# Tanh for SiLU, three scores ahead, and work moved between blocks in a hybrid decoder layer

## The reference, cut to what matters

```
h = x*(1+sc1) + sh1                      # adaLN; sh, sc, gt from c @ w_ada + b_ada
qkv_a, z_a, b_a, a_a, q_b, k_b, v_b, f_b, g_a, g_b = split(h @ w_in)
qkv_a = silu(causal_conv4(qkv_a))        # branch A: gated delta net, 8 heads of 64
q_a, k_a = l2norm(q_a)/8, l2norm(k_a);  o_a = gdn(...);  o_a = rmsnorm(o_a)*silu(z_a)
o_b = softmax(q_b.k_b/8 + F_t - F_s) v_b # branch B: forgetting attention, causal
merged = sigmoid(g_a)*(o_a @ w_ba) + sigmoid(g_b)*(o_b @ w_bb)
x = layernorm(alpha*x + gt1*(merged @ w_out));  h2 = x*(1+sc2) + sh2
x = layernorm(alpha*x + gt2*moe(h2))     # 64 experts, top 8, and a shared one
```

## Time and profile before

| | us |
|---|---|
| median of three runs | 1819.17 |
| profiled execution | 1827.16 |
| its span, first to last instruction | 1825.4 |
| TensorE busy in the span | 1644.6 (90%) |
| VectorE, ScalarE, GpSimd busy | 668.7, 340.9, 323.0 |
| mean granted clock of TensorE | 0.945 of full speed |
| attention block, 163.9 to 340.3 | 176.4 |
| sample-attention block, 340.3 to 487.8 | 147.5 |
| norms block, 487.8 to 512.0 | 24.2 |
| delta-net block, 512.0 to 869.6 | 357.6 |
| gated-norm block, 869.6 to 887.7 | 18.1 |
| gating block, 887.7 to 958.3 | 70.6 |
| output block up to the expert loop, 958.3 to 1142.5 | 184.2 |
| expert loop and end, 1142.5 to 1825 | 682.5 |

### The profile page before, as it was taken

One profiled execution on the slowest core, in us unless ns is written; L12 is line 12 of the kernel. 1 busy time (PEld: TensorE's weight loads), 2 busy tenths in 40 slices (PEclk: granted clock), 3 DMA queues, 4 the chain that ended last, 5 costly groups with the idle time before them and its releaser, 6 DMA issues. The chain is left out here.

```text
span 1825.4 us, 19720 instructions
## 1 busy us (share of the span) xinstructions
PE 1644.6 (90%) x7369; PEld 952.1 (52%) x7369; DVE 668.7 (37%) x1267; ACT 340.9 (19%) x680; POOL 323.0 (18%) x338
## 2 busy tenths in 40 slices
PE   5998889999768979999688987999999999999966
PEld 3856566664347667777563443444444444444422
DVE  2001332342477483442554963331111111111128
ACT  1001333433222121222110220111111111111120
POOL 5000000000049990000000240111111111111100
PEclk9997899999888989999798988999999999999989
DMA  9213010113131315130914004999999999989756
GB/s 342 81 46 107 17 47 1 47 59 104 50 96 53 113 54 133 60 114 15 354 65 155 35 4 166 408 421 394 368 405 397 399 370 406 408 352 420 303 194 262
DMA packets 113404, 357.09 MB, mean 196 GB/s; under 512 B 37739, under 2 KB 37867, under 8 KB 87187
## 3 DMA queue, kind: packets, MB, share of 16 engines
q1 hardware_dynamic: 88582, 304.08, 43.5%
q0 software_dynamic: 16112, 35.89, 5.1%
q10 hardware_dynamic: 8614, 15.84, 2.4%
HBM read 333.84 MB, written 40.79 MB: 205 GB/s over the span
## 5 line engine op out<-in xcount | busy, mean ns | idle before, releaser
L1833 PE MATMUL bank<-arena 128*64 128x512 f32 (+1 forms) x1152 | 366.8, 594 | 0.0
L1833 PEld LDWEIGHTS bank<-arena 128*64 128x64 f32 (+1 forms) x1152 | 139.0, 160 | 190.4 <-issue 190.4
L1841 PE MATMUL bank<-arena 128*64 128x512 f32 (+1 forms) x576 | 190.3, 599 | 0.9 <-DVE arena L2527 0.9
L1183 PE MATMUL bank<-arena 128*128 128x272 f32 x512 | 129.5, 403 | 20.2 <-PEq L1045 19.2
L2521 DVE TENSOR_TENSOR arena<-arena,bank 128x256 f32<-128x256 f32 x52 | 21.9, 421 | 329.5 <-ACT arena L2201 329.5
L1820 POOL DMA_INDIRECT expert_rows<-arena x52 | 52.5, 1010 | 494.1 <-PE bank L1826 439.6
L424 PE MATMUL bank<-arena 128*128 128x512 f32 (+4 forms) x384 | 127.3, 492 | 9.2 <-DVE arena L2330 6.9
L416 PE MATMUL bank<-arena 128*128 128x272 f32 x512 | 124.2, 407 | 11.0 <-DVE arena L1710 5.0
L1841 PEld LDWEIGHTS bank<-arena 128*64 128x64 f32 (+1 forms) x576 | 68.1, 160 | 117.9 <-issue 116.8
L1183 PEld LDWEIGHTS bank<-arena 128*128 128x128 f32 x512 | 95.4, 193 | 44.5 <-issue 21.8
L416 PEld LDWEIGHTS bank<-arena 128*128 128x128 f32 x512 | 101.2, 198 | 33.3 <-issue 6.1
(11 more groups left out here) (423 smaller groups left out, 2121.0 us busy)
## 6 DMA issues: line engine op xcount, KB each, us to landing
arena<-in_w_gate SPq DMA_DIRECT2D x64, 1024.0 KB
arena<-in_w_up SPq DMA_DIRECT2D x64, 1024.0 KB
arena<-in_w_down SPq DMA_DIRECT2D x64, 1024.0 KB
arena<-in_w_ada SPq DMA_DIRECT2D x12, 2048.0 KB, 9.6
arena<-in_w_in SPq DMA_DIRECT2D x11, 2048.0 KB, 9.0
arena<-expert_rows SPq DMA_DIRECT2D x8, 2048.0 KB, 25.2
gate_logits<-arena ACTq DMA_DIRECT2D x16, 272.0 KB, 2.9
arena<-gate_logits SPq DMA_DIRECT2D x8, 544.0 KB, 5.8
```

The lines of the kernel that those rows point to most:

```text
L1183: mm = nc.tensor.matmul(out[:, 0:HALF], w[:, k, m * P:(m + 1) * P], hT[:, k, half * HALF:(half + 1) * HALF], start=k == 0, stop=k == KD - 1)
L1833: mm = nc.tensor.matmul(out[rows].rearrange("p (a n) -> p a n", a=2), x[:, k, rows], gate_up_slot(n)[:, :, k, :], start=k == 0, stop=k == ...
L1841: mm = nc.tensor.matmul(out[rows, :], h[:, k, rows], down_slot(n)[:, k, 512 * half:512 * half + 512], start=k == 0, stop=k == 1)
```

## The change

1. Attention block: the scores are made three jobs ahead, in banks 0, 1 and 7; the other groups turn in banks 5 and 6. For feature tiles 0 to 5 SiLU is computed as u(1 + tanh u) with u half of the convolution; the taps of these tiles are halved once (`hist_half`), ScalarE takes tanh at j%4 == 0 two tiles later, VectorE multiplies (`conv_gate`) at j%4 == 1, and `conv_rows` goes from j%4 == 1 to j%4 == 2. Tile 6 keeps `conv_silu`, now the last work of ScalarE in the block.
2. Norms block: twelve filler pieces run on TensorE behind the transposes, and SP sends slab 2 there once the first "raw" piece is done. A tile of the delta-net block has 17 pieces instead of 20.
3. Branch weights b are loaded by SP in the delta-net block, between the sample output and slab 8, behind a wait for all stores; the b products of m=0 and m=1 run at the head of the gated-norm block.
4. `later_modulation` is cut into six steps behind m=1 to m=6, the sample token values come last.
5. The second gate row gets its bias behind `layernorm(1)`.

```diff
+    def conv_tanh(act, m):
+        act.wait_ge(conv_sum.sem, m + 1)
+        if m:
+            act.wait_ge(conv_act.sem, m)
+        ach.inc(nc.scalar.activation(conv_e[:, 0:SEQ], post[m % 2], ACT.Tanh))
+        conv_th.inc(nc.scalar.activation(conv_e[:, SEQ:TOK], post_s[:, m, :], ACT.Tanh))
+    def conv_gate(dve, m):
+        step = chained(dve, vch)
+        dve.wait_ge(conv_th.sem, m + 1)
+        step(nc.vector.scalar_tensor_tensor(post[m % 2], conv_e[:, 0:SEQ], 1.0, post[m % 2], ALU.add, ALU.mult))
+        done(conv_act, nc.vector.scalar_tensor_tensor(post_s[:, m, :], conv_e[:, SEQ:TOK], 1.0, post_s[:, m, :], ALU.add, ALU.mult))
-    RING = (5, 6, 7)
+    RING, SB = (5, 6), (bank[0], bank[1], bank[7])
-                if j >= 2:
-                    pe.wait_ge(s_exp.sem, j - 1)
+                if j >= len(SB):
+                    pe.wait_ge(s_exp.sem, j - len(SB) + 1)
-                if j % 4 == 1 and m >= 2:
+                if j % 4 == 2 and m >= 2:
                     conv_rows(pe, m - 2, RING)
+                if m >= 2 and j % 4 == 1:
+                    conv_gate(dve, m - 2)
+            taps = histT[:, 0:HALVED, NH:NH + CONV]
+            hist_half.inc(nc.scalar.mul(taps, taps, 0.5))
-                if j % 4 == 3 and m >= 1:
-                    conv_silu(act, m - 1)
+                if j % 4 == 0 and m >= 2:
+                    conv_tanh(act, m - 2)
             take_oT(PT - 1)
+            conv_silu(act, HALVED)
...
+            later_pieces(pe, "squares", 6)          # norms block, TensorE
+            later_pieces(pe, "norms", 6)
+            later_out(act, "squares")               # ScalarE, before the decays and the square root
+            later_out(act, "norms")                 # ScalarE, after the square root
             load_later(sp, 1)
+            sp.wait_ge(fill_mm.sem, slab_end[1])
+            load_later(sp, 2)
...
-                later_pieces(pe, (t, "state before"), 2)
+                later_pieces(pe, (t, "state before"), 1)
-                later_pieces(pe, (t, "transposes"), 1)
-                    later_pieces(pe, (t, l), 2 if l == NL - 2 else 1)
+                    later_pieces(pe, (t, l), 1)
-            for j in range(2, 8):
+            for j in range(3, 8):
                 send_later(j)
...
+            sp.wait_ge(stored.sem, stored.n)
+            branch_in[1].inc(sp.dma_start(wbb, A["w_branch_b"][0].rearrange("(k p) n -> p k n", p=P)), 16)
             for j in range(8, len(LATER)):
                 send_later(j)
...
+                if t == 0:                          # gated-norm block, TensorE
+                    pe.wait_ge(branch_in[1].sem, 16)
+                    yb_mm.inc(feature_major(wbb, 0, oTb, bank[4:6], CW))
+                    yb_mm.inc(feature_major(wbb, 1, oTb, bank[6:8], CW))
...
+                    if w is wbb and m < 2:          # gating block, TensorE
+                        continue
-                if m == 2:
-                    later_modulation()
+                if 1 <= m <= 6:
+                    later_modulation(m - 1)
+            sample_token_values()
...
             layernorm(0)
             layernorm(1)
+            add_gate_bias(gt2_load, gt2b, b_gt2)
             choose(0)
```

More of the change, by code:

```diff
@@ L715, in prob_transposes @@
                 pT_mm.inc(mm)
-            scores(0)
-            scores(1)
+            for j in range(len(SB)):
+                scores(j)
             pe.wait_ge(hist_load.sem, 32)
@@ L1226, in _ @@
         def _(pe):
+            g4 = gdec[:, 0:PT, :]
+            nc.tensor.matmul(bank[0][:, 0:32], chunkU, g4, start=True, stop=True)
+            nc.tensor.matmul(bank[0][:, 32:64], chunk1, g4, start=True, stop=True)
+            for cc in range(2):
+                for par in range(2):
+                    nc.tensor.matmul(bank[2][64 * par:64 * par + 64, 16 * cc:16 * cc + 16], chunk1[:, 64 * cc:64 * cc + 64],
+                                     gdec[:, 0:PT, par::2], start=True, stop=True)
@@ new lines, in _ @@
+        @block.scalar
+        def _(act):
+            step = chained(act, ach)
+            step(nc.scalar.copy(ab[:, :, 0], beta[0:NS_TOK, PT, :]))
+            ab_done.inc(nc.scalar.activation(ab[:, :, 1], gdec[0:NS_TOK, PT, :], ACT.Exp))
+            act.wait_ge(cn_mm.sem, 1)
+            n = CONV - 1 + NH
+            for i in range(3):
+                cn_sb.inc(nc.scalar.copy(cnew_rows[:, 512 * i:512 * i + 512], bank[3 + i][0:n, :]))
+            later_out(act, "squares")
+            act.wait_ge(g_sb.sem, 1)
+            step(nc.scalar.activation(gam, G, ACT.Exp))
+            g_exp.inc(nc.scalar.activation(gs[:, 2:4], gs[:, 2:4], ACT.Exp))
+            act.wait_ge(sq_sum.sem, 1)
+            sq_root.inc(nc.scalar.activation(ss, ss, ACT.Sqrt))
+            later_out(act, "norms")
@@ new lines, in build @@
+    trT = at(X0 + 9472, 4, CW, P)
+    rows_of = [at(T1 + 6912, 4, W), at(T1 + 9472, 4, W)]
+    kd_of = [at(T2, W), at(T1 + 8960, W)]
+    LT, dec, Lm0, Tm, Um, P1 = (at(T2 + 512 + 1024 * i, H, P) for i in range(6))
+    Lm_of = [Lm0, at(X0 + 4096, H, P)]
+    S = at(T2 + 6656, CW, HD)
+    u = at(T2 + 6912, W)
+    sS, stmp = at(T1, HD, 32), at(T1 + 2048, HD, 32)
+    sx = at(X0 + 13696, DS, 3, HD)
+    sab, snab = at(X0 + 13696 + 768, DS, 2), at(X0 + 13696 + 776, DS)
+    sv, so, skv = at(X0 + 13696 + 784, DS, 32), at(X0 + 13696 + 912, DS, 32), at(X0 + 13696 + 1040, 32)
@@ L1227, in _ @@
+    w_mm, w1_sb, w2_sb, un_mm, un_sb, od_mm, st_sb2, o_sb = (Tick(nc, n) for n in (
+        "w_products", "w1_copied", "w2_copied", "state_read", "u_done", "o_product", "state_updated", "o_copied"))
+    srec, so_back = Tick(nc, "sample_recurrence"), Tick(nc, "sample_out_moved")
+    t_act = Tick(nc, "later_inverse_T_copied")
+    NL = 6
+    KK_BANK = (2, 3, 4, 5)
+    with nc.Block() as block:
+        @block.tensor
+        def _(pe):
             for t in range(PT):
@@ L2322, in layernorm @@
                     dve.wait_ge(x_back.sem, 32)
[L2323 to L2326 removed]
+                    add_gate_bias(gtb_load, gtb, b_gt)
                 for half in range(2):
```

179 lines of the change are left out of this document (74 added, 105 removed).

## The result

The changed kernel takes 1802.18 us (median of four runs, 1799.73 to 1802.98), the kernel before 1820.38 us beside it (four runs, 1817.45 to 1821.92): a ratio of 0.9892, with a 95% interval of 0.9873 to 0.9911, or 18.2 us less. I had forecast 1792, with a range of 1783 to 1804. The result lies in that range, near its slow end, and outside the 1787 to 1798 that I gave the forecast itself. The profiled execution of the changed kernel took 1799.73 us around a span of 1798.0, 27.4 less than the span of before. Of these 27.4, some 7 are not the change's (see the first experiment).

What follows compares the result with a forecast made beforehand. TensorE was taken as the bound: its work, its waits and half-speed stretches behind them. Attention -8.3, norms and delta-net -1, gated norm 0, gating -12.5, output -5.0 sum to -26.8 us: 1792 forecast, range 1783 to 1804.

Steps and rivals of the forecast that it cites:

- The stalls of the attention block: Six TensorE stalls on the exponential lose their table loads, -5.8 us; later conv_rows adds 0.9, the ring of two 0.7.
- The clock behind the stalls: Attention block: shorter stalls spare TensorE half-speed stretches, 5 us back, bounds 3.4 and 8.5.
- Three scores ahead: Attention block: no help with the stalls, the maximum queues behind conv_part; third scores at the start fill a weight wait, -1.0 us.
- (a): Delta-net tiles, one of two pieces stays between states and transposes: -2.2 us in tile 0, -1.0 each in tiles 2 and 3.
- (c): Delta-net tiles, one piece instead of two at inversion level 4: -1.8 us in tiles 0, 2 and 3, nothing in tile 1.
- (b): Delta-net tiles, piece behind the transposes gone: wait grows to 2.6 us, half-speed stretch 1.7 us; +6.8 over four tiles, 5 taken.
- Rival (1): The filler gives back: half-speed stretches in all tiles, SP's store wait, a late slab; +8 instead of -1, 1801 us; 18%.
- Gating block: Two products fewer, the 5.0 us stall and its slow restart gone, 2.4 us kept for late gates: -12.5 us.
- Output projection: Deferred bias additions remove TensorE's 6.87 us wait and slow restart; 2.47 us return before choose(0): -5.0, bounds -3 and -7.4.
- (2): Attention block: exp and tanh need a load each way, half of 10.8 us is lost, 1798 us; 5%.
- (3): More clock returned than counted: attention takes 3.5 us more, the filler 5 more, 1784 us; 17%.
- (4): Slower than before: several waits per tile keep TensorE at 1.2 GHz through the inversion levels, up to 1828 us; 5%.

Runs made afterwards that it cites:

- the first experiment: The kernel before, run again unchanged for a second profile (also written experiment 1): 1821.92 us, one run.
- experiment 8: Changed kernel with VectorE's maxima one job ahead, but SiLU by its own table as in the kernel before: 1812.29 us, ratio 0.9903.
- experiment 3: Changed kernel with VectorE taking the maximum of job j+1 before the convolution part of job j: 1781.33 us, ratio 0.9781.
- experiment 4: Changed kernel with scores two jobs ahead in two banks and a ring of three banks; tanh and the rest stay: 1808.15 us, ratio 0.9919.
- Experiment 9: Changed kernel with maxima one job ahead, scores in two banks and a ring of three: 1788.19 us, ratio 0.9774.
- experiment 2: Changed kernel with one filler piece per delta-net tile moved back behind the transposes, five instead of six behind the decay products: 1799.52 us, ratio 0.9863.
- experiment 5: The changed kernel again, unchanged, for a second profile on another chip: 1814.78 us, ratio 0.9923.
- experiment 10: Changed kernel with the second pair of gate-bias additions back in the first layernorm: 1820.86 us, ratio 0.9953.
- experiment 6: Changed kernel with the attention block of before (SiLU by table, two score banks, ring of three): 1814.34 us, ratio 0.9922.

## Why the prediction was right or wrong

**The stalls of the attention block: right.** (The six gains that I read, 1.2 to 0.5, add to 5.9 and not to 5.8.) Their sum fell from 17.7 to 12.3 us, and 1.2 us came on for the ring of two: 4.2 less, which is my 5.8 less 0.9 and 0.7 (the parts 5.4 and 1.2 against 4.9 and 0.7). The 1.0 us for the weights went, and the 1.9 at the end came: TensorE's wait ahead of the next block grew from 1.13 to 2.99. ScalarE has one table load up to the last SiLU. The Trainium skill (ScalarE: Activation LUTs, "Table sets: the hidden batching unit") says that exp and tanh share a set; this trace agrees. The drain of about 1.38 us that the same page ("What ACT_TABLE_LOAD costs") puts on top of a load is not there: in experiment 8 the load at 244.69 took 1.28 and the next ACTIVATE began at 245.98. My estimate by that page, some 16 us for six pairs, was also short: twelve loads with a drain each, at the page's 2.66, would be 32.

**The clock behind the stalls: the step that failed.** The premise was that a stall, once short enough, costs no half-speed stretch. I wrote "I take 5 us back, bounds 3.4 and 8.5". Nothing came back: TensorE's busy time grew by 1.8 us in the first profile and by 6.5 in the second. I had read one stall of 1.69 us that cost nothing as a threshold. In the new trace stalls of 2.06 and of 0.70 us cost 1.8 and 1.6, those of 0.52 and 0.69 nothing, and one slow part (3.40 us at 301.27) has no stall of its own in front. So the length of a stall alone does not set the loss; what does is open. Where the stalls vanished, in experiment 3, 10.5 to 15.2 us of busy time came back at once. The term is off by 6.8 us in the first profile and by 11.5 in the second; 1792.4 was too low by 9.8.

**Three scores ahead: right**, by experiment 4, and for the reason given: the maximum is late however early its scores exist. Experiment 9 goes beyond the reason: with the maxima ahead the third bank does not help either.

**Norms and delta-net: too much gain counted for (a) and (c).** The start came 1.7 us later in the first profile and 3.2 in the others, not 3.9. A half-speed stretch of (b) costs 3.2 us in tile 2 (0.9, 1.8 and 0.5 in its rows), not 1.7, but all four together cost the block only 5.6 (experiment 2), near my 5. What was mis-sized is what the missing pieces give. With the piece put back only (a) and (c) are left, and the block lasts 350.9 us against 355.2 in the kernel before on that chip: 4.3 us, where I had counted 9.7. From the products behind the copies of one tile (8x128) to those of the next it is 98.1, 92.4 and 79.2 us in experiment 1, 98.0, 95.7 and 79.2 in experiment 5, and 94.5, 99.8 and 75.5 in experiment 2. So tiles 0 and 2 gave more than I counted, and tile 1, for which I wrote 0, grew by 7.4: less work for TensorE turned into longer waits for VectorE there. On that chip +3.2 - 4.3 + 5.6 is +4.5 (measured +4.4), against my -1; in the first pair of profiles it is +1.0. Rival (1) is in part what happened: without this filler the kernel is 2 to 3 us faster.

**Gating block: right.** 59.2 us, inside the 56 to 60 that I named (61.3 in experiment 5, with waits of 0.63 and 1.86); no long wait, the second row tile's wait gone, the gates 8.6 us in.

**Output projection: too low by 1 to 3.** Measured 5.7 to 7.4 by the pair without the gap, 6.7 by the pair with it, 8.3 by experiment 10; I had -5.0, with a bound of -7.4. That the 2.5 us of the deferred additions, which I charged in full, are hidden after all would explain it; no run takes them apart.

**Sum.** -1.6 + 1.0 - 11.4 - 7.5 (the output block less the gap) and -1.0 in the sample-attention block and the start are -20.5 in the profiles, against -26.8. Of the shortfall, 6.7 is the attention block, and 2.5 too much for the output block hides a part of the rest. By medians the change is worth 18.2 us in the first set, 14.0 in the second and, with two score banks, 13.3 on the first chip of the experiments. So the forecast owes its place in the range partly to the width of that range. Rivals (2), (3) and (4) did not come: no load between exp and tanh, no clock returned, and in the inversion levels of tiles 2 and 3 sixteen products take 2.00 us, full speed.

## What to carry to other kernels

When a wait has two chains that end within about a microsecond of each other, taking away one shows nothing: find what is late next and cut both in one step, here the table loads and the order of the maxima. A shorter stall need not give any clock back, so a term for the clock belongs in a sum only where the stall disappears; and filler taken from behind one wait to cover another pays only if the first wait has something else to cover it. Compare blocks only between profiles of one chip, and look whether each profiled execution lies near the median of its runs: 4 us in one block and 7 in another came from the chip or the execution, not from the code, and in experiment 6 the profile lay 8 us above its median on the same chip.

## What the runs showed of the hardware that I had not expected

The same instruction order with all but the same waits cost 158.0 us of TensorE time in one profile of the changed attention block and 162.8 to 163.0 in four others (676 matmuls each), and that of before 156.3, 156.4 and 163.5 in three. A stall of 0.70 us was followed by matmuls at half speed and one of 1.69 us was not. And 64 small router products take 1.1 us on one chip and 7.5 on two others, with gaps for which the profile names no releaser.
